# Attention scores issued two tiles at a time in a fused transformer layer

## The reference, cut to what matters

```python
SEQ = 1024; CHUNK = 64; N_LEFT_CHUNKS = 8; HEAD_DIM = 64; N_HEADS = 8
...
scores = jnp.einsum('bcqhd,bckhd->bhcqk', qc, kb).astype(jnp.float32)
...
scores = jnp.where(valid[None, None, :, None, :], scores + bias[None, :, None], NEG_INF)
p = jax.nn.softmax(scores, axis=-1).astype(v.dtype)
o = jnp.einsum('bhcqk,bckhd->bcqhd', p, vb)
```

## Time and profile before

| what | value |
|---|---|
| median of 3 runs | 1126.9 us (1126.6 to 1126.94) |
| profiled execution, its own time | 1127.98 us |
| span of the profiled execution | 1126.2 us |
| mean granted TensorE clock | 1.0 |
| PE busy | 1113.9 us, 99% |
| DVE busy | 697.6 us, 62% |
| ACT busy | 460.0 us, 41% |
| POOL busy | 161.0 us, 14% |
| line 803 (scores), first to last start | 93.9 to 372.8 us |

### The profile page before, as it was taken

How to read it: one execution, slowest core, us unless ns; L and a number is a source line. 1 busy time by engine, 2 the same in 40 slices (tenths; PEclk the granted TensorE clock), 3 DMA queues, 4 the chain that set the end, 5 groups by cost and what they waited for, 6 DMA issues and landing times.

```text
span 1126.2 us, 16073 instructions
## 1 busy us (share of the span) xinstructions
PE 1113.9 (99%) x5736; PEld 923.6 (82%) x5736; DVE 697.6 (62%) x1164; ACT 460.0 (41%) x869; POOL 161.0 (14%) x259
## 2 busy tenths in 40 slices
PE   8999999999999999999999999999999999999997
PEld 7887887887887788888888888888888878888886
DVE  5314445436345657786878787777777767655584
ACT  5332442443545545663332323222323246544441
POOL 4200011001110112210122112211211120000031
PEclk9999999999999999999999999999999999999999
DMA  8220101110110155342564446444634579976632
GB/s 281 95 75 19 38 20 38 38 38 19 39 38 20 61 201 187 131 131 80 174 214 158 133 137 214 143 127 159 205 112 151 193 252 362 314 231 225 220 117 83
DMA packets 112215, 154.15 MB, mean 137 GB/s; under 512 B 6992, under 2 KB 72536, under 8 KB 112160
## 3 DMA queue, kind: packets, MB, share of 16 engines
q1 hardware_dynamic: 95584, 96.49, 26.7%
q0 software_dynamic: 15424, 52.74, 13.6%
q10 hardware_dynamic: 1152, 4.19, 0.9%
HBM read 113.26 MB, written 40.13 MB: 136 GB/s over the span
## 4 chain that ended last, share of the span: by engine, by line
PE 66%; DVE 1%; DMA 1%; ACT 0%; SPq 0%; issue 0%; DVEq 0%; ACTq 0%
PE psum L1132 34%; PE psum L1159 17%; PE psum L1022 7%; PE psum L788 5%; DMA raw<-in_w_ffn_out 1%; PE psum L777 1%; PE psum L832 1%; PE psum L813 0%; PE psum L803 0%; SPq L577 0%; SPq L571 0%; PE psum L937 0%; ACT sq_junk L1287 0%; DVE hT L2065 0%; DVE ws L1623 0%
## 5 line engine op out<-in xcount | busy, mean ns | idle before, releaser
L788 PE MATMUL psum<-hT,ws 128*128 128x512 f32 (+1 forms) x1104 | 254.0, 385 | 0.0
L788 PEld LDWEIGHTS psum<-hT,ws 128*128 128x128 f32 x1104 | 197.3, 188 | 38.9 <-issue 0.7
L1132 PE MATMUL psum<-arena_r,ws 128*128 128x512 f32 x960 | 224.1, 389 | 0.0
L1132 PEld LDWEIGHTS psum<-arena_r,ws 128*128 128x128 f32 x960 | 180.2, 188 | 37.4
L1132 PE MATMUL psum<-hT,ws 128*128 128x512 f32 x720 | 169.9, 389 | 0.0
L1132 PEld LDWEIGHTS psum<-hT,ws 128*128 128x128 f32 x720 | 135.1, 188 | 28.0
L1159 PE MATMUL psum<-hT 128*128 128x512 f32 (+1 forms) x600 | 135.6, 385 | 1.1 <-DVE hT L2065 1.1
L1159 PEld LDWEIGHTS psum<-hT 128*128 128x128 f32 x600 | 111.1, 188 | 24.3 <-DVE hT L2065 1.9
L1991 DVE TENSOR_TENSOR misc<-misc,psum 128x512 f32<-128x512 f32 x100 | 68.5, 685 | 48.7 <-PE psum L1132 46.1
L1498 ACT ACTIVATE ws<-o_raw 128x512 fp32r<-128x512 f32 x40 | 25.2, 631 | 138.5 <-DVE o_raw L1969 138.0
L1022 PE MATMUL psum<-ws,hT 128*128 128x512 f32 x348 | 81.5, 392 | 0.0
(11 more groups left out here) (211 smaller groups left out, 1359.5 us busy)
## 6 DMA issues: line engine op xcount, KB each, us to landing
raw<-in_w_ffn_in SPq DMA_DIRECT2D x44, 512.0 KB, 4.2
act_scratch<-arena POOLq DMA_DIRECT2D x77, 256.0 KB, 3.2
raw<-in_w_in SPq DMA_DIRECT2D x22, 512.0 KB, 3.8
arena<-in_w_ffn_out POOLq DMA_DIRECT2D x22, 512.0 KB, 5.8
arena<-act_scratch SPq DMA_DIRECT2D x38, 256.0 KB, 3.5
arena<-in_x SPq DMA_DIRECT2D x16, 512.0 KB, 5.7
raw<-in_w_out SPq DMA_DIRECT2D x16, 512.0 KB, 3.5
raw<-act_scratch SPq DMA_DIRECT2D x26, 256.0 KB, 3.5
```

The lines of the kernel that those rows point to most:

```text
L788: last = mm(PP[pair][:, at:end] if to is None else to, w[wp], hT[:, hp, k, at:end], start=(k == 0 and (wp, hp) == (0, 0)), stop=(k == KT - ...
L1132: last = mm(blocks(bank), w[:, k * P:(k + 1) * P], b_operand(i, part, k), start=fresh_bank and k == 0 and w is hi and part == 0, stop=k == ...
```

## The change

The scores of tiles 0 and 1 are issued together in step 0, those of tiles 2 and 3 together in step 2, and steps 1 and 3 issue none. Tiles 4 to 7 stay as they are. Tiles 1 and 3 (the odd ones below 4) go to the other bank of each head, at column 512. VectorE and ScalarE make all four units of the two tiles in steps 0 and 2. As tile 3 uses the buffers of tile 1, VectorE waits before unit 6 for the transposes of tile 1. TensorE waits explicitly, in steps 2 and 4, for ScalarE's read of the tile turned before.

```diff
         def scores_at(u):
-            return 128 if keys(u)[1] == BAND else 0
+            if keys(u)[1] == BAND:
+                return 128
+            return u // 2 % 2 * 512
+
+        def scored(s):
+            if s < 4:
+                return (s, s + 1) if s % 2 == 0 else ()
+            return (s,) if s < NT else ()
...
-                for at, end in ((start, min(start + max(n, 256), 512)), (512, start + n)):
-                    if at >= end:
-                        continue
+                pieces = ((start, 512), (512, start + n)) if n == BAND else ((start, start + max(n, 256)),)
+                for at, end in pieces:
...
-                if s < NT:
+                if scored(s):
                     if t == 0 and s == 0:
                         pe.wait_ge(proj_free, 2)
                     else:
                         pe.wait_ge(biased, unit(t, 2 * s))
-                    scores(t, s)
+                    for i in scored(s):
+                        scores(t, i)
                 if s > 0:
                     pe.wait_ge(exp_done, unit(t, 2 * s))
+                    if s in (2, 4):
+                        pe.wait_ge(pT_act, tile(t, s - 1))
...
-                    exp(t, 0)
-                    exp(t, 1)
+                    for u in range(4):
+                        exp(t, u)
                     if more:
                         high_in(chunk(t, BG))
...
                 read_pT(t, s - 1)
-                if s < NT:
-                    exp(t, 2 * s)
-                    exp(t, 2 * s + 1)
+                for i in scored(s):
+                    exp(t, 2 * i)
+                    exp(t, 2 * i + 1)
...
-                    add_bias(t, 0)
-                    add_bias(t, 1)
+                    for u in range(4):
+                        add_bias(t, u)
                     if more:
                         low_in(chunk(t, BG))
...
-                if s < NT:
-                    add_bias(t, 2 * s)
-                    add_bias(t, 2 * s + 1)
+                for i in scored(s):
+                    if i == 3:
+                        dve.wait_ge(pT_psum, tile(t, 2))
+                    add_bias(t, 2 * i)
+                    add_bias(t, 2 * i + 1)
```

## The result

Five executions of the changed kernel have a median of 1134.7 us, against 1126.9 before: a ratio of 1.006, 95% interval 1.0048 to 1.0072. It is slower, as forecast, but by 7.8 us where I forecast 3.9, and outside my range of 1129.0 to 1132.3. Four of the five lie between 1132.56 and 1135.81 us, while those of before lie within 0.4 us of each other, so there is scatter to explain as well (the fifth took 2212.51 us, a disturbed execution that nothing here explains and no comparison uses).

What follows compares the result with a forecast made beforehand. TensorE, busy in 99% of the span, was taken as the bound. Costs of 0.44 (pair 0), 0.48 each (pairs 1 and 2) and 2.49 (pair 3), together 3.9 us, moved 1126.9 to 1130.8 us; range 1129.0 to 1132.3.

Steps and rivals of the forecast that it cites:

- Together 3.9 us: Attention, all four pairs: 0.44 for pair 0, 0.48 each for pairs 1 and 2, 2.49 for pair 3.
- its first bound: If merged blocks save nothing, step 0 costs +0.55 instead of +0.36 us, plus part of steps 3: at most +0.6 us.
- the two waits of the earlier trace: TensorE's waits, taken as its two longest: 1.1 and 1.0 us, behind attention, for helpers that themselves wait for TensorE.
- What TensorE saves: Merged score blocks, two a pair: each second block 0.18 us cheaper, eight in all 1.5 us, at most 1.9.
- Step 1: Fill or transpose_o waits for helpers once the covering scores are gone: +0.36 us in pairs 0 and 3, +0.40 in 1 and 2.
- Steps 2 and 3, pairs 0 to 2: VectorE's taps end at 7.92 us, copy_o comes late, TensorE stalls 0.2 us before turn_back: +0.08 us a pair.
- Steps 2 and 3, pair 3: copy_o queues behind unit 7, its exponentials, high_in and low_in; turn_back comes 2.13 us later, TensorE stalls some 2.6 us.
- a tenth lower when run without gaps: Bound on unit, exponential and split prices: pair 3 loses 0.7 us less, pairs 1 and 2 0.3 less each.
- The clock: Rival: pair 3's stall lets TensorE's clock fall to 1.2 GHz, next fill +2.9 us, 1133.7 us; chance 0.08.
- the helpers are not late: Rival: read_half, copy_o and o_scale come in time everywhere, merges gain 1.5 to 1.9 us, 1125.2 us; chance 0.04.
- Absorption of 1 to 2 us: Rival: later waits of 1.0 and 1.1 us absorb this, or pair 3's stall is half as long; 1128.8 us; chance 0.12.
- the sign that I had set: Behind attention: the forecast counts as wrong if that stretch gets shorter; no size given.

Runs made afterwards that it cites:

- The last experiment: Against the changed kernel: tiles 0/1 merged only in pairs 1 and 2, tiles 2/3 in all pairs, helpers in old order, pair 3's low_in behind copy_o; 1125.2 us.
- steps 2 and 3 alone: Changed kernel with only tiles 2 and 3 issued together, tiles 0 and 1 as before the change; 1131.3 us, ratio 1.0033.
- pair 3 alone: Changed kernel with the change kept only in pair 3, pairs 0 to 2 as before; 1131.1 us, ratio 1.0034.
- the whole change again: The changed kernel without any edit, run once more beside the kernel before; 1134.7 us, ratio 1.0066.
- with the stall filled: Changed kernel plus, in pair 3 before the wait for the copy, ten 512-column products whose result is not used; 1132.5 us.
- helpers in the old order: Changed kernel with TensorE's merged scores kept, but VectorE and ScalarE making two units a step as before; 1127.17 us, ratio 1.000.

## Why the prediction was wrong

The place of every wait was right. What failed is the attention term, "Together 3.9 us", which measured 5.8 and alone puts the time above the range, and the clock, whose fall the forecast left to a rival with a chance of 0.08. The range itself had a slip: 1130.8 and the 0.6 us of its first bound make 1131.4, not 1131.7. And the two waits of the earlier trace rows are not TensorE's longest: three in the program's start, of 1.5, 1.2 and 1.1 us, were left out. Neither changes the sum.

*What TensorE saves: right.* 0.36 us was forecast for the second 256-column block and 0.35 measured; 0.71 + 0.71 for the two of step 2, and 1.41 measured. The last experiment cashed it in.

*Step 1: right in place and nearly in size.* Pair 0 +0.36, pair 3 +0.40 (0.36 forecast), pairs 1 and 2 +0.49 (0.40 forecast). Each wait is on the engine and line that I named.

*Steps 2 and 3, pairs 0 to 2: place right, size wrong.* The term "the 0.18 us of the merge is eaten by the taps: +0.08 us a pair" measured 0.26, 0.64 and 0.61. The count of VectorE's queue failed: I had the taps' end at 7.92 us into step 2, and in pair 1 it was 198.10 - 189.62 = 8.48. Of the 0.56 missing, 0.37 lie between units 4 and 5 (0.34 of them the issue gap), 0.04 between units 5 and 6 (with the new wait between them), 0.07 between units 6 and 7, and 0.08 from unit 7 to the end of the taps. The last two are one misreading, used twice: the 0.99 us of a 512-column unit, which the earlier trace rows have as 1.06 when they are counted from reduction to reduction. In pair 2 the late start, 0.35 us, is in front of unit 4. In pair 0, without the gap, the taps end at 8.10, and the 0.18 us over 7.92 are what the size was off by there. The experiment with steps 2 and 3 alone shows it without the gap: 0.26 in all three.

*Steps 2 and 3, pair 3: place right, 2.61 for 2.13.* The same causes: the gap once, the misread unit once, the new wait. That low_in in front of copy_o is the link was shown by moving it alone: 9.58 to 6.60 us.

*The sum of attention* is thus 5.8 and not 3.9 us. My bound, prices "a tenth lower when run without gaps", looked at one side only; none was lower. The medians of the experiments in which the clock did not fall lie 0.1 to 0.6 us lower against the kernel before than their stretches say. Where these tenths are was not found.

*The clock: the rival was real.* "The clock" had 0.08 of the chances, and I took the forecast as if it did not happen. It happens in some executions of the changed kernel. Shown: the granted clock at 0.50 at the stall's end or behind it in three profiles (pair 3 alone and steps 2 and 3 alone, with stalls of 2.6 us, and the whole change again, with 2.95), and at 1.00 throughout attention in every profile without a stall of over 2.5 us; with the stall filled, runs at 1132.3 to 1132.8 us only. Its price was 1.6 us in the profile that caught it with the whole change, against my 2.9. The two longest runs of the result, 1134.72 and 1135.81 us, had mean granted clocks of 0.997 and 0.995, where the two short ones had 0.999. The first is as long as the execution whose profile shows the low clock (1134.70); the second must have had it for longer. These 2 to 3 us are put down to the clock by their means, not by a trace of them.

Together: the 5.8 us of attention give the 1132.6 us of the shortest runs, and the clock the step from there to the median of 1134.7. The rival that the helpers are not late is dead for the kernel as it is, and true for a kernel with another order. Absorption of 1 to 2 us is not what the medians show, as the shortest runs carry the whole 5.8 us. But the sign that I had set, a shorter stretch behind attention, did appear in the profiles: 734.6 us for 736.2, with the wait of 1.1 us gone. As only one profile of the kernel before exists, it stays open how many of its executions hold this wait, and whether the 0.1 to 0.6 us above are its share.

## What to carry to other kernels

When the bounding engine has no idle time, its small blocks still serve as cover for the helpers: before merging or moving one, count the queue of each helper up to the instruction that the bounding engine needs next, with each wait for another engine in that queue, and make this count first for the shortest step. Batch the issue on the bounding engine and leave the helpers' order alone; if one stall remains, look for a long instruction in front of the short one that is waited for, as one moved line was worth 3 us here. And give a stall of some us its second price, the clock behind it, when it is the longest of the kernel.

## What the runs showed of the hardware that I had not expected

VectorE's list has gaps of 0.34 us marked "issue" at fixed places. In the kernel after they are between the memset and the reduction of unit 4 in pair 1 and of unit 5 in pair 3, and they are in both profiles of it, and in the variants that keep its count of instructions up to there. Counted in the trace from 0, with waits, these are the instructions 191 and 447 of VectorE, 256 apart; halfway between them, at 319, unit 4 of pair 2 starts 0.35 us later behind read_half than in pair 0 (1.10 us from start to start, not 0.75). In the kernels with another count of instructions in front (before, pair 3 alone, steps 2 and 3 alone, helpers in the old order), the same numbers fall within three instructions behind a 0.56 us reduction or on idle time, and no such gap shows. What the engine does there was not tested.

The clock does not have to fall inside a stall. In the whole change again it was at full speed when the stall of 2.95 us ended, and fell some 1 us later, in the middle of a busy fill. In the two profiles with stalls of 2.6 us it fell before turn_back. A stall of 2.95 us in the result's own profile left it at 1.00.
